# Moving one weight group of a gated-DeltaNet projection: q, z, z, k, v, v in place of z, z, q, k, v, v

## The reference

```python
proj = h @ w_in                                   # 2048 -> 12352 columns
qkv, z, b_logit, a_logit = jnp.split(proj, splits, axis=-1)
qkv = jax.nn.silu(causal_depthwise_conv(qkv, short_conv))      # width 4
q, k, v = jnp.split(qkv, [GDN_QK_WIDTH, 2 * GDN_QK_WIDTH], axis=-1)
q = l2_normalize(q...) * (GDN_HEAD_DIM ** -0.5);  k = l2_normalize(k...)
o = chunk_gated_delta_rule(q, k, v, g, beta)      # triangular solve, then the outputs
o = rms_norm(o, o_norm) * jax.nn.silu(zf)         # z is needed only here, at the end
return o.reshape(...) @ w_out
```

## Time and profile before

| | |
|---|---|
| median of 3 runs | 2852.75 us |
| lowest, highest | 2846.46, 2852.94 us |
| the profiled execution's own time | 2853.19 us |
| its span, first to last instruction | 2851.7 us |
| TensorE matmul busy | 2766.0 us, 97% |
| VectorE busy | 1882.2 us, 66% |
| ScalarE busy | 1403.6 us, 49% |
| GpSimd busy | 510.6 us, 18% |
| granted TensorE clock, mean | 0.983 |

### The profile page before, as it was taken

The page is one execution under the profiler, slowest core; times in us unless marked ns, Lnnn a source line. Parts: engine busy times, 40 slices in busy tenths (PEclk is TensorE's granted clock), DMA queues, the critical chain, the costliest instruction groups (busy, mean ns, idle before and its releaser), DMA issues. The chain is left out here.

```text
span 2851.7 us, 43744 instructions
## 1 busy us (share of the span) xinstructions
PE 2766.0 (97%) x15939; PEld 2427.1 (85%) x15939; DVE 1882.2 (66%) x2464; ACT 1403.6 (49%) x2137; POOL 510.6 (18%) x475
## 2 busy tenths in 40 slices
PE   8999999999999999998999999989999999999998
PEld 7878788888888888887988878869888888888887
DVE  4799675655655557678679678774765555555555
ACT  4577544444444444465473463744444444444444
POOL 0001151221211215111020110120432121111214
PEclk8999999999999999999999999999999999999999
DMA  5554355556555555455364444564455555555553
GB/s 183 177 178 147 117 181 189 191 184 194 185 189 192 184 183 176 159 208 165 127 210 155 168 149 146 192 185 144 163 192 191 191 185 184 192 191 192 181 176 130
DMA packets 246087, 501.20 MB, mean 176 GB/s; under 512 B 10919, under 2 KB 11528, under 8 KB 244648
## 3 DMA queue, kind: packets, MB, share of 16 engines
q1 hardware_dynamic: 237504, 473.99, 50.6%
q0 software_dynamic: 5616, 24.75, 2.7%
q10 hardware_dynamic: 2808, 0.38, 0.1%
HBM read 491.64 MB, written 7.44 MB: 175 GB/s over the span
## 5 line engine op out<-in xcount | busy, mean ns | idle before, releaser
L983 DVE TENSOR_TENSOR w_lo<-raw,w_hi 128x1024 fp32r<-128x1024 f32 (+1 forms) x912 | 1151.2, 1298 | 713.8 <-ACT w_hi L570 713.1
L570 ACT ACTIVATE w_hi<-raw 128x1024 fp32r<-128x1024 f32 (+1 forms) x912 | 906.9, 1037 | 935.5 <-PE acc L1848 917.1
L1855 PE MATMUL acc<-xs,w_hi 128*128 128x512 f32 x5120 | 1294.6, 400 | 46.1 <-DVE ut L989 22.2
L1855 PEld LDWEIGHTS acc<-xs,w_hi 128*128 128x128 f32 x5120 | 942.9, 191 | 233.5 <-DVE ut L989 24.3
L1848 PEld LDWEIGHTS acc<-xs,w_lo 128*128 128x128 f32 x5120 | 666.7, 191 | 34.6 <-DVE w_lo L983 4.5
L1848 PE MATMUL acc<-xs,w_lo 128*128 128x256 f32 x5120 | 689.5, 284 | 2.8 <-DVE w_lo L983 2.8
L1855 PE MATMUL acc<-hs,w_hi 128*128 128x512 f32 x1920 | 466.2, 391 | 4.5 <-ACT w_hi L570 4.5
L1855 PEld LDWEIGHTS acc<-hs,w_hi 128*128 128x128 f32 x1920 | 350.3, 188 | 71.5 <-ACT w_hi L570 5.3
L577 ACT ACTIVATE tmp<-acc 128x256 f32<-128x256 f32 x448 | 169.2, 383 | 278.9 <-PE acc L1848 212.1
L1848 PEld LDWEIGHTS acc<-hs,w_lo 128*128 128x128 f32 x1920 | 251.4, 191 | 12.5
L1848 PE MATMUL acc<-hs,w_lo 128*128 128x256 f32 x1920 | 255.2, 282 | 0.0
(11 more groups left out here) (300 smaller groups left out, 1598.0 us busy)
## 6 DMA issues: line engine op xcount, KB each, us to landing
raw<-in_w_in SPq DMA_DIRECT2D x136, 1024.0 KB, 5.2
raw<-in_w_gate SPq DMA_DIRECT2D x88, 1024.0 KB, 5.1
raw<-in_w_up SPq DMA_DIRECT2D x88, 1024.0 KB, 5.1
raw<-in_w_down SPq DMA_DIRECT2D x64, 1024.0 KB, 5.1
raw<-in_w_out SPq DMA_DIRECT2D x48, 1024.0 KB, 5.1
raw<-in_w_down SPq DMA_DIRECT2D x32, 768.0 KB, 4.4
L<-g_rows POOLq DMA_DIRECT2D x4, 1536.0 KB, 7.6
I<-g_rows POOLq DMA_DIRECT2D x4, 1536.0 KB, 7.4
```

The source lines that it names most:

```text
L570: nc.scalar.activation(w_hi[:, c % 2, k], raw[:, c, k], ACT.Copy).then_inc(hi_ready, 2 if kc == 1 else 1)
L983: nc.vector.tensor_tensor(w_lo[:, c % 2, k], raw[:, c, k], w_hi[:, c % 2, k].bitcast(F32), ALU.subtract).then_inc(lo_ready, 2 if kc == 1 e ...
L1855: mm(acc[:, m, :], w_hi[:, c % 2, k, cols], r[:, kk], start=kk == 0, stop=end, skip_group_check=True)
```

## The change

The q group, with the columns of set j+1, goes from place 2 to place 0 of a round; the two z groups go from places 0 and 1 to places 1 and 2; k, v0 and v1 stay. The convolution's index is taken from the list of groups that have one, since those are no longer neighbours. The wait of the z gate counts one silu more, for q's now comes ahead of both of z. The order in `in1_first` and `in1_last` stays, as do the places of the loads of `L` and `I`.

```diff
@@ -126,7 +126,7 @@
     segs += [Segment("in1_first", 1, qkv(0)),
-             Segment("in1", SETS - 1, z(0) + qkv(1), deltanet=True),
+             Segment("in1", SETS - 1, qkv(1)[:1] + z(0) + qkv(1)[1:], deltanet=True),
              Segment("in1_last", 1, z(SETS - 1) + [Group("out1", GW * n, "x", "resid", at=n) for n in range(4)],
@@ -1062,7 +1062,7 @@
                 n0 = 4 * here.conv
-                i, b = here.i, here.b - here.s.conv_of[0]
+                i, b = here.i, here.s.conv_of.index(here.b)
                 j = i + 1 if here.s.name == "in1" else 0
@@ -1549,7 +1549,7 @@
                 dve.wait_ge(gd_pe[a], NP * j + P_OT)
-                dve.wait_ge(conv_silu, 6 * j + 6)
+                dve.wait_ge(conv_silu, 6 * j + (6 if isinstance(j, int) and j == SETS - 1 else 7))
                 z = zs[:, 2 * a:2 * a + 2, :].rearrange("p b t -> p (b t)")
```

## The result

| | before | after |
|---|---|---|
| median of 5 runs | 2852.84 us | 2839.99 us |
| lowest, highest | 2846.46, 2854.68 | 2834.87, 2842.33 |
| the profiled execution's own time | 2853.19 | 2834.87 |
| its span | 2851.7 | 2833.3 |
| granted TensorE clock, mean | 0.983 | 0.988 |

The ratio is 0.9956, 95% interval 0.9945 to 0.9967. The medians differ by 12.9 us, and the interval of the ratio is 9.4 to 15.7 us.

What follows compares the result with a forecast made beforehand. VectorE's wait for `Lb`, then 34.1 us of VectorE, then TensorE were taken to pace a round. The terms, 0 for group 3, group 1 and the landing, left the median at 2852.7 us, range 2846 to 2859.

Steps and rivals of the forecast that it cites:

- the landing of `Lb`: On the DMA queues in group 1: the return of `L` through DRAM was taken to land unchanged, 0 us.
- first rival: On the queues, `Lb` lands sooner since `raw` is no longer ahead: 10.8 us at most, 2842.0; chance 0.06.
- sign of being wrong: Wrong if `Lb`'s landing moves over 3 us against the `L` products, the 34.1 us stretch changes, or groups 3 to 5 shorten.
- The bound of 10.8: Most that sooner landings of `Lb` could give over three rounds, taking the fastest landing of 4.0 us: 10.8 us less.
- The stores' 1.8 us: GpSimd's stores of `L` in group 1: no delay in the sum, `Lb` issued at 1303.10 us as before.
- VectorE's wait: Before line 1575 in group 1, for `Lb`: from 7.9, 7.6 and 7.3 us to about 4.8, 4.5 and 4.2.
- the 6.0 us: VectorE's convolution of q, moved from group 3 to group 1 each round, fits its idle time there: cost 0.
- The transposes: TensorE in group 1 waits 0.6, 0.2 and 0.9 us for `I` products, 1.7 us, hidden by its wait before group 2.
- Group 3: VectorE gets 6.0 us free there, but TensorE sets the pace: worth 0.
- The 34.1 us: Stretch from line 1575 to TensorE's last wait for group 2's sums, paced by VectorE: to stay at 34.1 us.
- The clock: TensorE's clock stays up around its wait before group 2: 2.7 us a round, 8.2 in all, 2844.5; chance 0.07.
- GpSimd held: Line 1075's convolution instructions on VectorE hold GpSimd's stores in group 1: 3.4 us more, 2856.1; chance 0.05.

Runs made afterwards that it cites:

- e4: The changed kernel, with the load of `raw` for chunk 3 of group 2 held until `Lb` lands in rounds 0 to 2; median 2841.58 us, ratio 0.9967.
- e6: The changed kernel, with the load of `raw` for chunk 2 of group 2 held until `Lb` lands, in all four sets; median 2834.97 us, ratio 0.9942.
- e5: The kernel before, with the load of `raw` for chunk 2 of group 2 held until `Lb` lands, in all four sets; median 2829.69 us, ratio 0.9921.
- e2: The changed kernel, with all eight pieces of q's convolution in one block behind group 1's fourth `I` product; median 2850.44 us, ratio 1.0000.
- e3: The changed kernel, with piece 5 of q's convolution moved behind the `w_lo` halves of chunk 3; median 2850.34 us, ratio 0.9996.
- e1: The kernel before, with the load of `raw` for chunk 3 of group 2 held until `Lb` lands in rounds 0 to 2; median 2840.67 us, ratio 0.9972.

## Why the prediction was wrong

**The step that failed** is the landing of `Lb` in the part on the queues: "I take 0". The prediction had the facts, that `raw` would move from beside `Lb` to behind it (1.6 us, measured 1.18), and the mechanism as its first rival. It gave that rival 0.06, on the argument that a later `raw` would overlap more of the second load. It was the other way round: the second load is issued 0.54 us behind the first, so before it stood behind `raw`, and now it stands ahead of it. With `raw` 1.2 us behind the first, both take 3.2 to 3.9 us. From issue to use the term was 8.68 - 4.33, 8.54 - 4.60 and 8.22 - 4.53, in all 12.0 us less. Against it stand 0.45 + 0.66 + 0.73 = 1.8 us by which the stores land later; together the two make the 10.1 us. The prediction's own sign of being wrong, a landing that moves against the `L` products by over 3 us, came in two of the three rounds and nearly in the third (3.9, 3.3 and 3.0 us from first store to use).

The bound of 10.8 was right in kind and a little small, as the three last landings fell by 4.3 + 3.6 + 3.3 = 11.2 us: its lower end, 4.0 us, came from a row with `raw` beside it. The prediction also looked at the rows of the three rounds, saw that they differ by 0.9 us, and left it there. With `raw` 0.06, 0.20 and 0.26 us behind, the last landing took 8.1, 7.5 and 7.2 us, which pointed down; the fourth set, 9.6 us at 0.13, doesn't fit, so the rows gave a sign and no size. Where the bounds are 10.8 less and 6.0 more and the change puts the big load behind the small one, 0.06 was far too little.

**The stores' 1.8 us** are a second term that the prediction put at nothing, with `Lb` issued "at 1303.10 as before". They land later where chunk 2's load of `raw` is issued 3.56 us after the first store and not 2.52. e4 keeps this (9.49 to 9.65 us) with chunk 3's load out of the way; e6, with chunk 2's also held, has 6.53, and e5 the same without the convolution. e2, where that load is back at 2.50 us, has 9.08. So VectorE's work alone doesn't delay the stores; the load beside them does.

**VectorE's wait** was to fall to 4.8, 4.5 and 4.2 us, and fell to 0.86, 1.14 and 1.09. With the landing's 4.35, 3.94 and 3.69 off and the stores' 0.45, 0.66 and 0.73 on, the forecast would have been 0.9, 1.2 and 1.2. The count of the 6.0 us and of where they go was right.

**The transposes** wait 0.37 and 0.66 us, and the third not at all: 1.03 for the 1.7 forecast. It was to be hidden in the wait before group 2, and that still is there with 0.47, 0.82 and 0.77 us, so the cover holds.

**Group 3** gave 0, as forecast: e2 has the same relief and a ratio of 1.0000. **The 34.1 us** are 34.12.

**The clock** was the other rival towards faster, at 8.2 us. Its first half came true, as the granted clock of the stretch is 1.00 for 0.90 and the wait ahead of it is below 1 us. It gave nothing, for the reason given against it: VectorE is busy 33.45 of the 34.12 us, and TensorE waits elsewhere. In that stretch it now waits 1.21 us for `w_lo` where it waited 0.41, and from 1180 to 2010 us these waits are 5.4 us for 2.2.

**GpSimd held**: the eight stores take 4.66 us for 4.68. Line 1075's work ends at 1286.01, only 0.26 us past the first store. e6 and e5, with and without the convolution in group 1, agree within 0.01 us from first store to `Lb`. The rule in the Trainium skill's "SBUF — State Buffer", section "SBUF: two separate sides", on VectorE starving GpSimd's descriptors, thus shows no cost here; with 0.26 us beside the stores it was hardly put to the test.

**Why 1.2 us is enough.** The two loads of `Lb` are issued 0.54 us apart. A gap of 0.01 to 0.47 us thus puts `raw` between them, and one of 0.94 us or more puts it behind both. Wherever it stood between them, in all rounds and all kernels, the second load landed within 0.2 us of `raw` itself: 8.65 and 8.70 us behind the first issue in round 0 of before, 7.51 and 7.35 in round 1 of e3. In after the second load has landed at 4.30 us and `raw` at 8.84. The first load goes by degrees: it lands after 5.8 to 6.7 us with `raw` up to 0.13 us behind, after 4.0 at 0.26 and after 3.5 at 0.33, which is what it takes in e1 with no `raw` beside it. Round 1 of e3, the `raw` load and both loads of `Lb`:

```profile
raw<-in_w_in SPq DMA_DIRECT2D x1, 1024.0 KB, 7.0
DMA to landing us min/median/max: 3.5/5.2/7.0
```

The edge then lies between 0.47 and 0.94 us. That it is the second issue, at 0.54, fits every row, but no run has a gap between the two, so it is argued and not shown; so is what goes on inside the DMA engines. The DMA engines' traffic in before (1302 to 1316 us, 40 slices) and after (1294 to 1304 us, 40 slices), busy tenths and GB/s:

```profile
DMA  0000007668999999999999643100000000000000
GB/s 0 0 0 0 0 0 88 70 181 281 334 439 363 234 228 234 246 246 322 380 287 211 135 117 100 47 0 0 0 0 0 0 0 0 0 0 0 0 0 0
```

```profile
DMA  2000000000898997996878998989986221000000
GB/s 90 0 0 0 0 0 0 0 0 0 262 262 279 361 262 229 303 197 139 172 205 319 352 352 311 369 344 385 377 311 197 98 98 41 25 25 25 25 33 0
```

After, the first bytes move at 1296.5, 1.2 us behind `Lb`'s issue, at 262 to 361 GB/s; at that pace the two loads' 0.52 MB are through in some 1.8 us, by 1298.3. With the same delay from its issue at 1296.46, `raw` would begin to move near 1297.7, by estimate with two thirds of `Lb` ahead of it. Before, both start together, and their 1.6 MB move in one block from 1304.1 to 1311.1. The Trainium skill's "DMA: Bandwidth & Descriptors", section "Queues, rings and completion order", says that each DMA engine takes turns between the queues that have work for it, a packet at a time. The trace agrees in part: in before both kinds of load move in one block, and the first load of `Lb` lands at 1309.1 us, 2 us ahead of the block's end. But equal turns alone don't give the second load's time. By 1308.4 us the block has moved twice the 0.52 MB of `Lb`, and the second load landed at 1311.8, with `raw`. The trace doesn't name the packets' order, so that part stays open.

## What to carry to other kernels

A small load on the critical path and a big prefetch on another queue share the DMA engines, so look at which is issued first and how far apart, for each load by itself: a change that moves only VectorE's work can shift this by a microsecond and gain or lose several. When a change comes out faster for a reason that isn't its own, take the reason alone and carry it further: held back on purpose, in the old order and for the stores too, `raw` gave 21.7 us, 6.3 of them in the fourth set, which the change doesn't touch, for the change's 12.9, and the new order then cost time. A term that no row shows and that is the one thing a change does to the path deserves a chance by its bounds, and not a 0.

## What the runs showed that was not expected

- The effect of the gap has a sharp edge. In rounds 0 to 2 `Lb` is in use 7.5 to 9.6 us after its issue with `raw` 0.01 to 0.47 us behind, and 4.3 to 5.1 us after it with `raw` 0.94 us behind or more (e6 aside, where VectorE comes late). With the shorter gaps the second load of `Lb` landed with `raw`, within 0.2 us.
- Of eight stores of 32 KB the last land much later beside a megabyte load issued 2.5 us after the first store: 8.8 to 9.1 us from the first store to the load behind the last landing, 6.5 us without it.
